# Attention times values: split single-pass products in four combinations of halves, or plain float32 in two column halves

## The reference

```
# first block, 8 query heads of 64, 2 key/value heads
s = einsum('bqkgd,bskd->bkgqs', qblk, k)
p = softmax(s, axis=-1)
o = einsum('bkgqs,bskd->bqkgd', p, v)

# second block, two mixers of 8 heads of 64
p  = softmax(where(valid, logit, -inf));   oa = einsum('bqhk,bqkhd->bqhd', p, vg)     # the 128 best keys
att = where(strict, exp(log_sigmoid(z) + after), 0); ob = einsum('bhqs,bshd->bqhd', att, v_b)  # stick breaking
```

## Time and profile before

| | us |
|---|---|
| median of 3 runs | 1446.86 (1446.62 to 1446.95) |
| the profiled execution | 1446.43 |
| its span, first to last instruction | 1444.6 |
| PE busy | 1380.3 |
| PE weight loads busy | 1158.4 |
| DVE busy | 820.5 |
| ACT busy | 650.9 |
| POOL busy | 714.2 |
| mean granted TensorE clock | 0.984 of full |

### The profile page before, as it was taken

How to read it: one execution, slowest core, us unless ns; L and a number is a source line. 1 busy time by engine, 2 the same in 40 slices (tenths; PEclk the granted TensorE clock), 3 DMA queues, 4 the chain that set the end, 5 groups by cost and what they waited for, 6 DMA issues and landing times.

```text
span 1444.6 us, 18061 instructions
## 1 busy us (share of the span) xinstructions
PE 1380.3 (96%) x7167; PEld 1158.4 (80%) x7167; DVE 820.5 (57%) x1349; ACT 650.9 (45%) x1203; POOL 714.2 (49%) x380
## 2 busy tenths in 40 slices
PE   6889888999999999999999999999999999999998
PEld 6667678988888888887877877888889888888886
DVE  5569956676767665546777976542357421312224
ACT  5456716444431332634777665456454431323231
POOL 1248834456655554553333454338815664645560
PEclk8899998999999999999999999999999999999999
DMA  8313353355555454311111211114211222222321
GB/s 326 141 64 110 125 191 130 117 204 204 176 203 204 175 204 139 138 59 60 59 59 61 86 59 59 59 59 146 90 57 59 88 88 93 95 105 88 115 89 59
DMA packets 32052, 167.58 MB, mean 116 GB/s; under 512 B 3552, under 2 KB 4192, under 8 KB 18912
## 3 DMA queue, kind: packets, MB, share of 16 engines
q1 hardware_dynamic: 31968, 166.42, 32.8%
HBM read 164.31 MB, written 2.10 MB: 115 GB/s over the span
## 4 chain that ended last, share of the span: by engine, by line
PE 81%; DVE 9%; ACT 4%; POOL 2%; DMA 1%; issue 1%; SPq 0%; DVEq 0%; ACTq 0%
PE B L551 79%; POOL WL L2336 1%; ACT WH L1193 1%; PE B L972 1%; DMA ZF<-in_w_ada_rows 1%; PE B L795 1%; DVE SC L1790 1%; DVE ZF L1867 1%; DVE SC L2187 1%; DVE SC L1959 1%; DMA SC<-in_w_ada 1%; DVE ZF L2162 1%; DVE ZF L1876 1%; DVE M L2160 0%; DVE SC L1954 0%
## 5 line engine op out<-in xcount | busy, mean ns | idle before, releaser
L2336 POOL TENSOR_TENSOR WL<-RAW,WH 128x512 fp32r<-128x512 f32 (+1 forms) x197 | 473.1, 2416 | 486.5 <-ACT WH L1193 442.1
L551 PE MATMUL B<-HH,WH 128*128 128x512 f32 (+2 forms) x1040 | 405.0, 392 | 5.7 <-POOL HL L2348 2.4
L551 PE MATMUL B<-HH,WL 128*128 128x512 f32 (+2 forms) x1040 | 398.6, 386 | 0.0
L551 PE MATMUL B<-HL,WH 128*128 128x512 f32 (+2 forms) x1040 | 387.3, 384 | 0.0
L1193 ACT ACTIVATE WH<-RAW 128x512 fp32r<-128x512 f32 (+1 forms) x197 | 191.8, 1004 | 193.8 <-PE B L551 178.3
L551 PEld LDWEIGHTS B<-HH,WH 128*128 128x128 f32 x1040 | 197.6, 190 | 45.5 <-issue 4.3
L551 PEld LDWEIGHTS B<-HH,WL 128*128 128x128 f32 x1040 | 197.3, 190 | 39.2
L551 PEld LDWEIGHTS B<-HL,WH 128*128 128x128 f32 x1040 | 192.5, 189 | 34.9
L551 PE MATMUL B<-ZR 128*128 128x256 f32 (+4 forms) x1048 | 151.0, 326 | 19.9 <-ACT SC L1356 6.3
L551 PE MATMUL B<-ZR,WH 128*128 128x512 f32 (+1 forms) x624 | 164.7, 352 | 0.7 <-POOL WL L2336 0.7
L551 PEld LDWEIGHTS B<-ZR 128*128 128x128 f32 (+1 forms) x1048 | 120.4, 190 | 48.7 <-issue 14.8
(11 more groups left out here) (250 smaller groups left out, 1762.5 us busy)
## 6 DMA issues: line engine op xcount, KB each, us to landing
RAW<-in_slabs SPq DMA_DIRECT2D x102, 1024.0 KB, 4.9
ZF<-in_w_ada_rows SPq DMA_DIRECT2D x80, 512.0 KB, 4.1
G<-in_w_ada SPq DMA_DIRECT2D x8, 512.0 KB, 10.3
RAW<-in_slabs SPq DMA_DIRECT2D x4, 768.0 KB, 4.5
RAW<-in_x SPq DMA_DIRECT2D x4, 512.0 KB, 7.5
SC<-in_w_ada SPq DMA_DIRECT2D x4, 512.0 KB, 10.0
ZF<-in_w_ada SPq DMA_DIRECT2D x4, 512.0 KB, 10.1
out<-SC SPq DMA_DIRECT2D x8, 256.0 KB, 2.1
```

The costliest lines, as they stand in the source:

```text
L551: return e.matmul(out, l, r, start=start, stop=stop)
L2336: e.tensor_tensor(lo[:, at], k.RAW[:, i % 2, at], hi[:, at].bitcast(F32), ALU.subtract).then_inc(*w.hit((i, q)))
```

## The change

Probabilities and values are kept as plain float32, in `V1`, `PT1`, `V2` and `PT2`, which lie as float32 tensors over the same memory as parts of `ZR`. There are no low parts of them any more. The product of a head with a key block is one float32 matmul with the head's 64 columns of V as the stationary operand. It writes PSUM partitions 0 to 63 for the first head and 64 to 127 for the second, and the loop goes over key blocks outside and over the two heads inside. In the second block the last key block is multiplied for the second query block alone (128 columns), and `PT2` is kept twice. ACT's copy frees the PSUM bank of a turned unit and of V, and the output of a pair of heads is copied by one instruction of 128 partitions on ACT and one on DVE.

```
-        self.VH, self.VL = ([ZR[:, i + 512 * h:i + 512 * h + 512] for h in range(2)] for i in (1024, 2048))
-        self.PT1 = ZR[:, 7168:15360].rearrange("p (i h a j n) -> p i h a j n", i=2, h=2, a=2, j=4)
+        self.V1 = plain("V1", 1024, 512)[:, :]
+        self.PT1 = plain("PT1", 7168, 4096)[:, :].rearrange("p (i h j n) -> p i h j n", i=2, h=2, j=4)
...
+        self.V2 = plain("V2", 9216, 1024)[:, :]
+        self.PT2 = plain("PT2", 11264, 4096)[:, :].rearrange("p (i h j n) -> p i h j n", i=2, h=2, j=4)
...
+            def plain(name, first, n):
+                return nc.alloc_sbuf_tensor_at(name, [128, n], F32, offset=at + 4 * first)
... (PE, first block)
-            pe.wait_ge(v_mix["lo", u, 1])
-            for half in range(2):
-                for j in range(4):
-                    at = slice(128 * j, 128 * j + 128)
-                    t = mm3(b[:, 256 * i:256 * i + 256], k.VH[half][:, at], k.VL[half][:, at],
-                            k.PT1[:, u // 2 % 2, half, 0, j, :], k.PT1[:, u // 2 % 2, half, 1, j, :],
-                            half == j == 0, half == 1 and j == 3)
+            pe.wait_ge(a_mix["th", u, 1])
+            for j in range(4):
+                for half in range(2):
+                    at = 128 * j + 64 * half
+                    t = mm(b[64 * half:64 * half + 64, 256 * i:256 * i + 256], k.V1[:, at:at + 64],
+                           k.PT1[:, u // 2 % 2, half, j, :], j == 0, j == 3)
... (PE, second block)
-            pe.wait_ge(v_mix["lo2", u])
-            for half in range(2):
-                for j in range(blk + 1):
-                    at = range(4)[KEYS[blk]][j]
-                    t = mm3(b[:, 256 * half:256 * half + 256], vp[:, 128 * j:128 * j + 128], vp[:, 512 + 128 * j:640 + 128 * j],
-                            k.PT2[:, half, 0, at, :], k.PT2[:, half, 1, at, :], j == 0, j == blk)
+            pe.wait_ge(a_mix["th2", u])
+            for j in range(blk + 1):
+                for half in range(2):
+                    v, n0 = 512 * (c % 2) + 128 * j + 64 * half, 128 if j == blk else 0
+                    t = mm(b[64 * half:64 * half + 64, n0:256], k.V2[:, v:v + 64], k.PT2[:, u // 4 % 2, half, j, n0:256],
+                           j == 0, j == blk)
... (ACT: zeros of V and of PT2 gone; V copied once; th and th2 free the bank)
-            if u > 3:
-                act.wait_ge(weigh_full["o2", u // 4 - 1])
+            if u > 7:
+                act.wait_ge(weigh_full["o2", u // 4 - 2])
...
-            for half in range(2):
-                r = slice(64 * half, 64 * half + 64)
-                dst = k.OAH[3][r, at] if key == "a" and c == 3 else (k.OBH if key == "b" else k.OA)[r, c, at]
-                e.activation(dst, B["o2", h][r, 256 * half:256 * half + 256], ACT.Copy).then_inc(*mix.hit(("oh2", h)))
+            dst = k.OAH[3][:, at] if key == "a" and c == 3 else (k.OBH if key == "b" else k.OA)[:, c, at]
+            e.activation(dst, B["o2", h][:, 0:256], ACT.Copy).then_inc(*mix.hit(("oh2", h)))
... (DVE: "vl", "lo", vlo and "lo2" gone, such as)
-                dve.wait_ge(a_mix["th", u, half])
-                e.tensor_tensor(lo, B["t1", u, half][:, :].rearrange("p (j n) -> p j n", j=4), hi.bitcast(F32),
-                                ALU.subtract).then_inc(*mix.hit(("lo", u, half)))
-                B.free(("t1", u, half), mix["lo", u, half])
...
+            e.tensor_tensor(lo, B["o2", h][:, 0:256], hi.bitcast(F32), ALU.subtract).then_inc(*mix.hit(("ob", h)))
```

More of the change, by code:

```diff
@@ L1266, in act_program @@
     xt(5), xt(7)
-    for half in range(2):
-        for v in (k.VH, k.VL):
-            e.activation(heads_of(v[half])[1 - half], heads_of(k.CST[:, 0:512])[0], ACT.Copy, scale=0.0).then_inc(
-                *mix.hit("fill"))
     weights()
@@ L1333, in act_program @@
     act.wait_ge(tok_full["v"])
-    for half in range(2):
-        e.activation(heads_of(k.VH[half])[half], heads_of(B["tok", "v"][:, :])[half], ACT.Copy).then_inc(*mix.hit(("vh", half)))
+    e.activation(k.V1, B["tok", "v"][:, :], ACT.Copy).then_inc(*mix.hit("v1"))
+    B.free(("tok", "v"), mix["v1"])
     for s in range(STEPS1):
@@ L1472, in masks @@
             e.activation(dst, src, ACT.Copy)
-        for half in range(2):
-            e.activation(k.PT2[:, half, :, 3, 0:128], k.CST[:, 0:256].rearrange("p (a n) -> p a n", a=2), ACT.Copy, scale=0.0)
         e.activation(k.SNR[:, 0:128], k.STN, ACT.Copy, scale=0.0)
@@ L1498, in vhi @@
         act.wait_ge(vp_free(k, x))
-        e.activation(vp_of(k, x)[0], B["tok", x][:, :], ACT.Copy).then_inc(*mix.hit(("vh", x)))
+        e.activation(v2_of(k, x), B["tok", x][:, :], ACT.Copy).then_inc(*mix.hit(("vh", x)))
+        B.free(("tok", x), mix["vh", x])
     act.wait_ge(v_mix["rot", "ki"])
@@ L1967, in dve_program @@
     head_newton("q1")
-    dve.wait_ge(a_mix["vh", 1])
-    for half in range(2):
-        e.tensor_tensor(heads_of(k.VL[half])[half], heads_of(B["tok", "v"][:, :])[half],
-                        heads_of(k.VH[half].bitcast(F32))[half], ALU.subtract).then_inc(*mix.hit("vl"))
-    B.free(("tok", "v"), mix["vl"])
     for s in range(STEPS1):
@@ L1987, in dve_program @@
             e.reciprocal(k.INV[:, u, :], k.SUM[:, u, :]).then_inc(*mix.hit(("inv", u)))
-        u = at1(s, "lo")
-        if u is not None:
-            at = slice(128 * (u % 2), 128 * (u % 2) + 128)
-            for half in range(2):
-                hi, lo = (k.PT1[:, u // 2 % 2, half, i, :, at] for i in range(2))
-                dve.wait_ge(a_mix["th", u, half])
-                e.tensor_tensor(lo, B["t1", u, half][:, :].rearrange("p (j n) -> p j n", j=4), hi.bitcast(F32),
-                                ALU.subtract).then_inc(*mix.hit(("lo", u, half)))
-                B.free(("t1", u, half), mix["lo", u, half])
         u = at1(s, "out")
@@ L2170, in dve_program @@
     for s in range(STEPS2):
-        for x, t in TURN_V.items():
-            if s - 1 == t and x in ORDER2:
-                vlo(x)
-        u = at2(s, "lo")
-        if u is not None:
-            blk = UNITS2[u][3]
-            hi, lo = (k.PT2[:, u % 2, i, KEYS[blk], 128 * (blk % 2):128 * (blk % 2) + 128] for i in range(2))
-            dve.wait_ge(a_mix["th2", u])
-            e.tensor_tensor(lo, B["t2", u][:, 0:128 * (blk + 1)].rearrange("p (j n) -> p j n", j=blk + 1), hi.bitcast(F32),
-                            ALU.subtract).then_inc(*mix.hit(("lo2", u)))
-            B.free(("t2", u), mix["lo2", u])
         u = at2(s, "z", 0, 31)
@@ L2209, in dve_program @@
             dve.wait_ge(a_mix["oh2", h])
-            for half in range(2):
-                r = slice(64 * half, 64 * half + 64)
-                hi, lo = (k.OBH[r, c, at], k.OBL[r, c, at]) if key == "b" else (k.OAH[3][r, at], k.OAL[3][r, at])
-                e.tensor_tensor(lo, B["o2", h][r, 256 * half:256 * half + 256], hi.bitcast(F32), ALU.subtract).then_inc(
-                    *mix.hit(("ob", h)))
+            hi, lo = (k.OBH[:, c, at], k.OBL[:, c, at]) if key == "b" else (k.OAH[3][:, at], k.OAL[3][:, at])
+            e.tensor_tensor(lo, B["o2", h][:, 0:256], hi.bitcast(F32), ALU.subtract).then_inc(*mix.hit(("ob", h)))
             B.free(("o2", h), mix["ob", h])
```

33 lines of the change are left out of this document (11 added, 22 removed).

## The result

| | before | after |
|---|---|---|
| median, us | 1446.9 (4 runs beside the kernel after) | 1425.8 (1424.81 to 1426.92, 4 runs) |
| profiled execution, span | 1446.43, 1444.6 | 1425.82, 1424.0 |

The ratio is 0.9856, with a 95% interval of 0.9844 to 0.9868: 21.1 us less, where 1431 was forecast and 1424 was the lower end.

What follows compares the result with a forecast made beforehand. PE was taken to bound the kernel, with 81% of the chain. 11.4 us from PE plus 5.0 from stalls, 16.4 off 1446.43, gave 1430.0, as median 1431 us; range 1424 to 1455, the likeliest case's own 1424 to 1439.

Steps and rivals of the forecast that it cites:

- the overlap: In PE's weighings, two column halves run at once: 0.216 us a 256-column product, against 0.432 if never; chance 0.52.
- the split: Around each weighing, changing the array to half columns and back costs 0.35 us, bounds 0 and twice that.
- The PE term: Shorter weighings on the chain in both attentions: 3.5, 6.3 and 1.6 us by kind, 11.4 us in all.
- The stalls: DVE and ACT work removed from the chain in both attentions: 10.0 us together, half counted, 5 us; bounds 0 and 10.
- L1994's 1.2 us: First attention: this removed DVE instruction stood on the chain with 1.8% of 65 us, 1.2 us.
- SP's and POOL's lists stay, and their events come as early as PE allows: Whole kernel: no DMA is moved and there are no new waits, so no loss was counted here.
- the likeliest case: Whole kernel: the halves overlap as forecast, giving 1431 us, own range 1424 to 1439; chance 0.52.
- No overlap: Rival at the weighings: column halves don't run at once, 0.432 us a product, +8 us, 1454 us; chance 0.27.
- Weight loads exposed: Rival at the weighings: loads wait for the other half's records, 0.326 us a full product, 1441 us; chance 0.12.
- Another engine keeps the time: Rival: DVE leads from 786 to 818 us and POOL from 158 on, so 8 us remain, 1438 us; chance 0.06.
- The signs named beforehand: Trace checks: weighing length, starts of the heads' records, DVE and ACT busy time, and shrinkage of both attentions' stretches.

Runs made afterwards that it cites:

- copies_kept: Kernel after, with the second attention's output copied in two halves on ACT and DVE and ACT waiting as if `PT2` were kept once: 1426.4 us, ratio 0.9863.
- lo_kept: Kernel after, with DVE's low-part subtractions of the probabilities put back, PE waiting for them and the banks freed by them: 1426.56 us, ratio 0.9858.
- relief: Kernel before without DVE's low parts of the probabilities, the second of three matmuls taking the high part again: 1441.83 us, ratio 0.9968.
- first_only: Kernel before with the change in the first attention alone: 1443.83 us, ratio 0.9981.
- second_only: Kernel before with the change in the second attention alone: 1426.82 us, ratio 0.987.
- full_width2: Kernel after, but second-block products take all 128 columns of V, one head after the other, with no column halves: 1440.39 us, ratio 0.9954.
- serial: Kernel after with each weighing's two loops swapped, all key blocks of one head before the other's: 1435.75 us, ratio 0.9929.

## Why the prediction was right, and where its sizes were off

**The step that decided, the overlap, was right, and better than forecast.** Products on half the columns run two at a time at 0.216 us a record. I had let the first record run alone; it doesn't (nor does the last), so a weighing takes 8 steps of a pair, 6 and 2 short ones, or 2 and 2 short ones, and not one more. With 0.30 for the split instead of 0.35, a weighing costs 1.73 + 0.30 = 2.03, 1.51 + 0.30 = 1.81 and 0.65 + 0.30 = 0.95 us where 2.29, 2.08 and 1.21 were forecast. The gains are 0.85, 1.06 and 0.48 instead of 0.58, 0.79 and 0.23. The PE term is then, by the prediction's own count of weighings, 6 x 0.85 + 8 x 1.06 + 7 x 0.48 = 16.9 us, not 11.4. **This is the term that was mis-sized**: 0.22 + 0.05 us in each of 21 weighings, 5.5 us in all.

**The stalls.** 5 us were put on DVE and ACT, of 10; the runs show 7.1. The second segment holds seven weighings of either kind (two more follow it), so 7 x 1.06 + 7 x 0.48 = 10.8 of its 16.7 us are PE's work and 5.9 are stalls. Two runs account for them: copies_kept loses 3.6, with the wait for ACT's exponential back (1.1 to 3.1), and lo_kept 1.8; relief, with PE's work as before, gains 2.4. PE's recorded idle time fell by only 4.1 us; the rest isn't in its gaps. In the first attention 6 x 0.85 = 5.1 us were to come from PE. The steps show 4.9 where 1.4 went to the lower clock and 6.3 in the two profiles where it didn't, so 1.2 are stalls, and relief gains 1.3 there. The share taken from the earlier trace rows, L1994's 1.2 us, was right.

**What was not foreseen** is of two kinds. Behind the first attention 2.9 us are given back, by a longer lead of POOL (1.4), by PE at the lower clock (0.85) and by pieces of w_ada paced by their DMA. "SP's and POOL's lists stay, and their events come as early as PE allows" was true of the lists; it overlooked that DVE, relieved, runs its pieces at other times, and that they and POOL's work slow each other. first_only, second_only and lo_kept show this in the lead: 25.2, 23.8 and 23.7 us. And the clock, which the prediction has nowhere, took 1.4 us in the first attention.

**The sum.** The first attention has 5.1 + 1.2 - 1.4, the way behind it -2.9, the second 10.8 + 5.9; with 0.25 at the start and 1.2 + 0.4 between and behind the attentions that is some 20.6, which is what the profiled executions show (20.60). The forecast 11.4 + 5.0 = 16.4 was 4.2 short. Some 8.5 us more were gained than forecast (4.9 by PE's work, 2.1 by stalls, 1.5 at the start and between), and 4.3 were lost that the prediction put at nothing. That the time fell inside the likeliest case's own range, 1.8 us above its lower end, owes something to these losses: the mechanism was right, the nearness partly luck.

**The rivals.** *No overlap* is excluded by the starts, and full_width2 measured its price: 3.03 and 1.305 us a weighing, where 3.02 and 1.30 were forecast for the work without the split's cost. *Weight loads exposed* is excluded too: the loads of a weighing run inside the time of its matmuls, and a pair of matmuls, each with weights of its own, starts 5 to 7 ns apart. The Trainium skill's rule (TensorE: Matmul & The Clock Gate, Part 3, The mechanism), by which loads run beside matmuls in flight only where the rows differ, is contradicted by this trace for column halves. Its other rule (TensorEngine Tiling (Array Packing), Tiling Modes, Key Properties), that a change of mode drains the engine, fits the trace, with 0.30 us for both ways. *Another engine keeps the time* is what happened behind the first attention, by POOL and the pieces of w_ada for some 2 of the 2.9 us, and not in the second.

**The signs named beforehand.** The weighing of 16 records was to last about 2.1 us: 1.88 with its way out. The second head's record was to follow the *second* of the first head's within a few ns: it follows the first. DVE was to fall by some 60 us: 61.8; ACT by a few: 11.2. The first attention with POOL's lead was to shrink by 3 to 5 us: 80.86 to 181.91 became 80.61 to 178.95, 2.7, for the reasons just given. From 700 to 973 us it was to shrink by 10 to 13: it was 16.7.

## What to carry to other kernels

Two products that each need only half the columns of the array cost the time of one, if their matmuls stand alternately in the program; with eight records in a row on one side, half of the overlap was lost. So count a split product in pairs of records plus 0.3 us a section, and put sections of different splits next to each other (0.15 us less for each). Before reading a segment's difference, compare the granted clock of both: 3.4 us at the lower level hid a fifth of the first attention's gain. When an engine off the path is relieved, ask what it will do earlier and who shares its time: here the answer was worth 1.4 us and more, and moving DMA-paced pieces was worth more than the relief.

## What the runs showed of the hardware that was not expected

- PE starts a matmul of the free half past up to three queued ones of the busy half (`serial`: the second head's first record 5 ns after the first head's fifth of eight).
- A POOL subtraction of 128x512 takes 1.26 to 1.31 us alone and up to 2.27 beside DVE's 128x1024 piece of w_ada, and such a piece 1.28 alone and up to 2.32 beside one of them. Other DVE instructions with two operands in SBUF slow it too (29 of 75 over 1.35 us); those that read PSUM or a single SBUF operand hardly do (2 of 77).
- The way from half columns to half rows costs no more than the way back to the full array (0.203 us from the last record), which saves 0.15 us where two such sections adjoin. The way into half columns costs 0.09 us behind a transpose and behind a 512-column matmul alike.
- After 5.15 us of idleness PE's matmuls came 0.43 us apart, at half its clock, from the second on (granted 0.50 since 177.3 us, within the idle time); after 2.40 us three steps still came at 0.23 before the clock fell. The same first attention ran at the full clock in two profiles and with 3.4 us at half of it in others.
